# Running the last output blocks and the first input units token tile by token tile between the parts of a macaron decoder layer

## What is computed

```python
def sandwich(x, fn, g_pre, g_post, shift, scale, gate, res_w):
    h = rms_norm(x, g_pre) * (1.0 + scale[:, None]) + shift[:, None]
    y = rms_norm(fn(h), g_post)
    return x + res_w * gate[:, None] * y

x = sandwich(x, lambda h: swiglu(h, ffn1_w_in[l], ffn1_w_out[l]), ...)
x = sandwich(x, lambda h: token_mixer(h, ...), ...)      # attention, sparse attention, retention
x = sandwich(x, lambda h: swiglu(h, ffn2_w_in[l], ffn2_w_out[l]), ...)
```

## Time and profile before

| | |
|---|---|
| three runs | 2011.61, 2013.59, 2013.87 us, median 2013.59 us |
| the profiled execution | 2008.18 us, its span 2006.1 us |
| TensorE busy | 1903.8 us, 95% of the span |
| VectorE busy | 1413.9 us, 70% |
| ScalarE busy | 825.3 us, 41% |
| mean granted clock of TensorE | 0.976 |

### The profile page before, as it was taken

The page is one execution under the profiler, slowest core; times in us unless marked ns, Lnnn a source line. Parts: engine busy times, 40 slices in busy tenths (PEclk is TensorE's granted clock), DMA queues, the critical chain, the costliest instruction groups (busy, mean ns, idle before and its releaser), DMA issues.

```text
span 2006.1 us, 21422 instructions
## 1 busy us (share of the span) xinstructions
PE 1903.8 (95%) x8610; PEld 1549.7 (77%) x8610; DVE 1413.9 (70%) x1474; ACT 825.3 (41%) x1019; POOL 20.0 (1%) x24
## 2 busy tenths in 40 slices
PE   2779999999999999899999999899999999999996
PEld 2558878878878788777777787788888888888895
DVE  5997888888878878765766567656656665555556
ACT  2224434443444343344565534443444444443442
POOL 0000000000000000000000000000000000000000
PEclk6789999999999999999999999999999999999998
DMA  9889988989989989435333435366666665555551
GB/s 347 321 313 351 354 338 324 357 325 343 346 322 347 347 327 340 162 114 184 126 115 129 156 133 187 135 243 231 246 243 232 235 218 189 189 189 189 195 194 73
DMA packets 204129, 486.82 MB, mean 243 GB/s; under 512 B 8048, under 2 KB 21120, under 8 KB 188928
## 3 DMA queue, kind: packets, MB, share of 16 engines
q1 hardware_dynamic: 202816, 482.79, 66.4%
q10 hardware_dynamic: 992, 2.63, 0.4%
...
...
## 4 chain that ended last, share of the span: by engine, by line
PE 49%; issue 38%; DVE 6%; DMA 2%; ACT 1%; POOL 0%; SPq 0%; POOLq 0%; DVEq 0%; ACTq 0%
PE ps_u L1328 6%; PE ps_g L1328 6%; PE ps_u L1330 5%; PE ps_u L1329 5%; PE ps_g L1330 5%; PE ps_g L1329 5%; DMA ada_raw<-in_ada_w 2%; DVE arena L1086 2%; PE ps_t L1328 2%; PE ps_t L1329 2%; PE ps_t L1330 2%; PE ps_y L1328 2%; PE ps_y L1330 2%; PE ps_y L1329 2%; DVE w_lo L812 1%
## 5 line engine op out<-in xcount | busy, mean ns | idle before, releaser
L812 DVE TENSOR_TENSOR w_lo<-w_raw,w_hi 128x1024 fp32r<-128x1024 f32 (+1 forms) x632 | 753.0, 1200 | 491.0 <-ACT w_hi L485 489.9
L485 ACT ACTIVATE w_hi<-w_raw 128x1024 fp32r<-128x1024 f32 (+1 forms) x632 | 657.2, 1042 | 944.6 <-PE ps_u L1330 336.1
L1328 PE MATMUL ps_u<-w_hi,xT_hi 128*128 128x512 f32 (+2 forms) x880 | 349.5, 397 | 19.5 <-DVE w_lo L812 18.7
L1328 PE MATMUL ps_g<-w_hi,xT_hi 128*128 128x512 f32 (+1 forms) x880 | 347.5, 395 | 18.4 <-DVE w_lo L812 9.6
L1329 PE MATMUL ps_u<-w_lo,xT_hi 128*128 128x512 f32 (+2 forms) x880 | 342.5, 389 | 0.0
L1330 PE MATMUL ps_u<-w_hi,xT_lo 128*128 128x512 f32 (+2 forms) x880 | 342.4, 389 | 0.0
L1330 PE MATMUL ps_g<-w_hi,xT_lo 128*128 128x512 f32 (+1 forms) x880 | 342.2, 389 | 0.0
L1329 PE MATMUL ps_g<-w_lo,xT_hi 128*128 128x512 f32 (+1 forms) x880 | 341.8, 388 | 0.0
L836 DVE SCALAR_TENSOR_TENSOR arena<-ada_raw,cond,arena 128x2048 f32<-128x2048 f32 x108 | 253.4, 2346 | 19.1 <-DMA ada_raw<-in_ada_w 19.0
L1328 PEld LDWEIGHTS ps_g<-w_hi,xT_hi 128*128 128x128 f32 x880 | 166.5, 189 | 61.0 <-issue 15.8
L1328 PEld LDWEIGHTS ps_u<-w_hi,xT_hi 128*128 128x128 f32 x880 | 167.7, 191 | 58.6 <-DVE w_lo L812 22.2
...
## 6 DMA issues: line engine op xcount, KB each, us to landing
w_raw<-in_ffn_w_in SPq DMA_DIRECT2D x160, 1024.0 KB, 5.0
ada_raw<-in_ada_w SPq DMA_DIRECT2D x128, 1024.0 KB, 7.1
w_raw<-in_ffn_w_out SPq DMA_DIRECT2D x80, 1024.0 KB, 5.0
w_raw<-in_mix_w_in SPq DMA_DIRECT2D x32, 1024.0 KB, 5.0
arena<-in_ada_w SPq DMA_DIRECT2D x16, 1024.0 KB, 10.2
w_raw<-in_mix_w_out SPq DMA_DIRECT2D x16, 1024.0 KB, 5.0
...
```

Of the source, the lines that this page charges most:

```text
L485: nc.scalar.activation(w_hi[:, u % 4, 0:n, 0:width], w_raw[:, s, 2 * hf:2 * hf + n, 0:width], ACT.Copy).then_inc(hi_done, 1)
L812: nc.vector.tensor_tensor(w_lo[:, u % 4, 0:n, 0:width], w_raw[:, s, 2 * hf:2 * hf + n, 0:width], w_hi[:, u % 4, 0:n, 0:width].bitcast(F32) ...
L1328: nc.tensor.matmul(o, a_hi[:, k, rows], w_hi[:, b, c, 0:width], start=start, stop=False)
```

## The change

The last two output blocks of a part (b = 2, 3) are computed for tile 0 of both, then for tile 1 of both (`last_blocks`), and the first four units of the next part's first group for tile 0, then for tile 1 (`first_group`). The norm steps of a turn are done per tile in one function `turn` on ScalarE and one on VectorE. The transposes of x come as eight pieces of 128 tokens for the first half of the chunks (`x_part`, `xt_part`) and as pairs for the second half. Scale and shift move from VectorE (L1021) to ScalarE: two activations with a scale and a bias column each, from PSUM into `junk`, then after a wait on its own semaphore a copy into `xT_hi` (`scaled`, `xt_hi_part`, `xt_hi_pair`). The identity matmuls become 20, then 16 after the first square of x. The last hidden block of a feed-forward part is transposed after output block 1 of the group before, into `ps_g`, and its split lands in `xT_hi` and `xT_lo`. The powers are four per turn instead of two (two instead of one at the end).

```diff
+            def xt_hi_part(n, b, t):
+
+                if b == 0 and t == 0:
+                    act.wait_ge(modcol_done, STRIPS + 2 * n)
+                    act.wait_ge(ysq_done, SQ_PART * n)
+                act.wait_ge(xt_done, 8 * n + 2 * t + b // 2 + 1)
+                raw = raw_part(b, t)
+                scaled(n, b, raw, xt_part(b, t), P)
+                nc.scalar.activation(xT_hi[:, 2 * b:2 * b + 2, t * P:(t + 1) * P], raw.rearrange("p (c n) -> p c n", n=P),
+                                     ACT.Copy).then_inc(xt_hi_done, 1)
...
+            def turn(n, y0, g, width):
+
+                sq = SQ_PART * n
+                for b in range(2):
+                    act.wait_ge(y_added, y0 + b + 1)
+                    y_square(n, b, 0, 2 * b)
+                    y_square(n, b, 1, 2 * b + 1).then_inc(ysq_done, 1)
+                act.wait_ge(ysq_done, sq + 2)
+                for b in (2, 3):
+                    act.wait_ge(y_first, 2 * n + b - 1)
+                    y_square(n, b, 0, b - 2).then_inc(ysq_done, 1)
+                if g is not None:
+                    hi_group(g, 4, width, None, range(0, 1))
+                    x_square(n + 1, 0, 0)
+                    x_square(n + 1, 0, 1)
+                for b in (2, 3):
+                    act.wait_ge(y_added, y0 + b + 1)
+                    y_square(n, b, 1, b).then_inc(ysq_done, 1)
+                if g is None:
+                    return
+                hi_group(g, 4, width, None, range(1, 2))
+                xt_hi_part(n + 1, 0, 0)
+                xt_hi_part(n + 1, 1, 0)
+                hi_group(g, 4, width, None, range(2, 3))
+                x_square(n + 1, 1, 0)
+                xt_hi_part(n + 1, 2, 0)
+                x_square(n + 1, 1, 1)
+                hi_group(g, 4, width, None, range(3, 4))
+                xt_hi_part(n + 1, 3, 0)
                 for b in range(4):
-                    xt_hi_later(n, b)()
+                    xt_hi_part(n + 1, b, 1)
+                for b in range(4, 8):
+                    hi_group(g, 4, width, None, range(b, b + 1))
+                    xt_hi_pair(n + 1, b)
 
 
...
@@ -925,7 +969,7 @@
                 last = FBLOCKS - 1
                 hidden(last, g0 + 5 + 3 * LOOP, TAIL)
                 yl, gy = y0 + 4 * last, g0 + 8 + 3 * LOOP
-                tail = {0: [y_add(gy - 1, yl - 2, 2)], 2: [y_add(gy - 1, yl - 1, 3)], 3: [ht_lo(j0 + last, TAIL // P)],
+                tail = {0: [ht_lo(j0 + last, TAIL // P, xT_hi, xT_lo, ps_g), y_add(gy - 1, yl - 2, 2)], 2: [y_add(gy - 1, yl - 1, 3)],
                         4: [gates(2 * f, 1 if f == 0 else 3, 0.5)], 5: [y_add(gy, yl, 0)], 7: [y_add(gy, yl + 1, 1)]}
                 lo_group(gy, TAIL // P, NB, tail)
...
-                    lo_group(g_next, 4, NB, None, range(0, 1))
-                y_add(g, y0 + 2, 2, False, pairs)()
-                if g_next is not None:
-                    lo_group(g_next, 4, NB, None, range(1, 2))
-                gated(2)
-                if g_next is not None:
-                    lo_group(g_next, 4, NB, None, range(2, 3))
-                last = slice(3 * NB, 4 * NB)
-                dve.wait_ge(y_added, y0 + 3)
-                dve.wait_ge(pe_half, n + 1)
-                nc.vector.tensor_tensor(yacc[:, 0, last], pairs[1][:, 0, :], yacc[:, 0, last], ALU.add).then_inc(y_first, 1)
-                dve.wait_ge(pe_used, 8 * g + 8)
-                nc.vector.tensor_tensor(yacc[:, 1, last], pairs[1][:, 1, :], yacc[:, 1, last], ALU.add).then_inc(y_added, 1)
-                dve.wait_ge(ysq_done, 4 * n + 4)
-                link(nc.vector.reduce_sum(ss[:, 0:2], ssy[:, :, :], AX_X))
-                nc.vector.tensor_scalar(ss[:, 0:2], ss[:, 0:2], 1.0 / D, EPS, ALU.mult, ALU.add).then_inc(var_ready, 1)
-                norms[0] += 1
-                gated(3)
-                dve.wait_ge(rstd_ready, norms[0])
-                dve.wait_ge(y_gated, 4 * n + 4)
-                for t in range(TILES):
-                    for part in range(2):
-                        cols = slice(part * D // 2, (part + 1) * D // 2)
-                        nc.vector.scalar_tensor_tensor(x_sb[:, t, cols], yacc[:, t, cols], rstd[:, t:t + 1], x_sb[:, t, cols],
-                                                       ALU.mult, ALU.add).then_inc(x_new, 1)
+                last_add(2, 0)
+                gated(2, 0)
+                last_add(3, 0)
+                dve.wait_ge(ysq_done, sq + 4)
+                y_first_ready = variance(0, ssy[:, 0:1, :])
+                gated(3, 0)
+                x_update(0, 0, y_first_ready)
+                x_update(0, 1, y_first_ready)
+                last_add(2, 1)
+                last_add(3, 1)
+                if gn is None:
+                    gated(2, 1)
+                    dve.wait_ge(ysq_done, sq + 6)
+                    y_second_ready = variance(1, ssy[:, 1:2, :])
+                    gated(3, 1)
+                    x_update(1, 0, y_second_ready)
+                    x_update(1, 1, y_second_ready)
+                    return
+                dve.wait_ge(xsq_done, 2 + 4 * n + 2)
+                x_first_ready = variance(2, ssx[:, 0:1, :])
+                gated(2, 1)
+                x_normal(0, 0, x_first_ready)
+                dve.wait_ge(ysq_done, sq + 6)
+                y_second_ready = variance(1, ssy[:, 1:2, :])
+                lo_group(gn, 4, width, None, range(0, 1))
+                gated(3, 1)
+                xt_rest(0, 0)
+                x_update(1, 0, y_second_ready)
+                lo_group(gn, 4, width, None, range(1, 2))
+                xt_rest(1, 0)
+                x_update(1, 1, y_second_ready)
+                lo_group(gn, 4, width, None, range(2, 3))
+                xt_rest(2, 0)
+                dve.wait_ge(xsq_done, 2 + 4 * n + 4)
+                x_second_ready = variance(3, ssx[:, 1:2, :])
+                lo_group(gn, 4, width, None, range(3, 4))
+                x_normal(1, 0, x_second_ready)
+                xt_rest(3, 0)
+                x_normal(0, 1, x_first_ready)
+                x_normal(1, 1, x_second_ready)
+                for b in range(4):
+                    xt_rest(b, 1)
+                for b in range(4, 8):
+                    lo_group(gn, 4, width, None, range(b, b + 1))
+                    xt_rest(b)
 
             def input_scale(n, meanwhile=None):
...
+            def last_blocks(g, a_hi, a_lo, chunk0, chunks, y0, pairs):
+
+                for t in range(TILES):
+                    for n in (2, 3):
+                        ps = pairs[n % 2]
+                        if t == 0:
+                            pe.wait_ge(y_added, y0 + n - 1)
+                        for hf in range(2):
+                            m = min(2, chunks - 2 * hf)
+                            pe.wait_ge(lo_done, 8 * g + 2 * n + hf + 1)
+                            ins = half_unit(a_hi, a_lo, chunk0 + 2 * hf, (2 * n + hf) % 4, m, NB, ps[:, t, :], t, hf == 0, hf == 1)
+                            if t == 1:
+                                ins.then_inc(pe_used, 1)
+                            elif hf == 1:
+                                ins.then_inc(pe_half, 1)
...
+            def x_part(n, t):
+
+                pe.wait_ge(xn_ready, 4 * (n - 1) + t + 1)
+                for b in range(4):
+                    for c in range(2):
+                        k = 2 * b + c
+                        ins = nc.tensor.transpose(xt_part(b, t)[:, c * P:(c + 1) * P], yacc[:, t, k * P:(k + 1) * P], ident[:, :])
+                    if b % 2:
+                        ins.then_inc(xt_done, 1)
...
+            def first_group(n, g, width, ps, ps_warm):
+
+
                 pe.wait_ge(gates_ready, n)
-                warm(24, ps)
-                pe.wait_ge(x_new, 4 * (n - 1) + 1)
-                warm(18, ps)
-                pe.wait_ge(xsq_done, 2 + 4 * n)
-                warm(8, ps)
-                for b in range(3):
-                    x_pair(n, b)()
-
-            def xt_pairs(n):
-                return {b - 3: [x_pair(n, b)] for b in range(3, 8)}
+                warm(20, ps_warm)
+                pe.wait_ge(xsq_done, 2 + 4 * (n - 1) + 1)
+                warm(16, ps_warm)
+                x_part(n, 0)
+                for t in range(TILES):
+                    for b in range(4):
+                        if t == 0 and b == 3:
+                            x_part(n, 1)
+                        if t == 0:
+                            pe.wait_ge(lo_done, 8 * g + b + 1)
+                        pe.wait_ge(xt_lo_done, xt_count(n, b, t))
+                        ins = half_unit(xT_hi, xT_lo, 2 * b, b, 2, width, ps[:, t, 0:width], t, b == 0, False)
+                        if t == 1:
+                            ins.then_inc(pe_used, 1)
+                            x_pair(n, 4 + b)
+                for b in range(4, 8):
+                    pe.wait_ge(lo_done, 8 * g + b + 1)
+                    pe.wait_ge(xt_lo_done, xt_count(n, b))
```

(12 more changed lines are left out.)

301 lines of the change are left out of this document (136 added, 165 removed).

## The result

The changed kernel takes 1992.33 us (median of 4 runs, 1989.65 to 1994.62) against 2012.6 us for the kernel before on the same chip (4 runs): a ratio of 0.9898, 95% interval 0.9886 to 0.991. It is 20.3 us faster. The forecast was 1997.8 us with a range from 1993.5, so the direction and the places were right, but the time lies 5.5 us under the forecast and 1.2 us under the range. The profiled execution took 1992.25 us, its span is 1990.5 us.

What follows compares the result with a forecast made beforehand. TensorE, busy 95% of the span, bounds the kernel except in a few places. First turn -9.5, second -5.6, end -0.7, together -15.8 us: 2008.18 becomes 1992.4 profiled, 1997.8 us on the median; range 1993.5 to 2003.5.

Steps and rivals of the forecast that it cites:

- the early transposes: Both feed-forward tails: transposing the last hidden block earlier removes the wait for `hT_lo`, gain 1.9 us each.
- the wait for block 1's add: Last output blocks: new TensorE wait before block 3 of tile 0, 0.8 us first turn, 1.0 to 1.1 second.
- the identity matmuls, not the norm, set the start: After the last block: 72 identity matmuls, 8.3 us, delay the transposes; in the first turn both end within 0.7 us.
- from the blocks' end: Last block to first weight matmul: 10.9 us instead of 20.81 and 19.07, so -9.9 and -8.2 us.
- The overlaps of neighbours: Overlaps within one queue, left out, about 0.9 us a turn; held against one half-speed stretch in one turn (1.7).
- VectorE's last chain: Kernel end, block 1's add to last update: 18.0 us, or 17.8 with some overlap, against 16.62 before.
- A pair of scaled activations: ScalarE, before the first weight matmul: two activations with scale and bias columns, 0.48 us each, 0.96 together.
- The three waits in the group: First group, tile 0 half: TensorE waits 1.5 us twice, then 1.3; group 29.0 us, +1.5 each turn.
- the clock's second case: Clock rival: neither turn pays for a half-speed stretch and overlaps count, 1996.0 us; no separate chance given.
- The case with 1994.5 us: Neither turn pays for the clock, activations at their lower bound, 0.75 us a turn less; 1993 to 1995.8, chance 0.20.
- both turns pay: Clock rival: half-speed stretches cost time in both turns, 1999.8 us; dearer activations or this, 2000 to 2003.5, chance 0.17.
- on the median, 5.41 us above it: Base of the sum: the median lies 5.41 us above the profiled execution, turning 1992.4 into 1997.8 us.

## Why the forecast missed the time, and what of it held

The bound, the places and the mechanism held. Of the steps by their own numbers: the early transposes gave 1.95 us in each tail for 1.9; the wait for block 1's add cost 0.82 and 1.13 for 0.8 and 1.0 to 1.1; the identity matmuls, not the norm, set the start in both turns, which the runs with fewer of them show (3.0 us gained in the second turn); from the blocks' end it was 10.61 us for 10.9; VectorE paced tile 0's half.

The failed step is in the sum: "The overlaps of neighbours that I left out, about 0.9 us a turn, are held against one such stretch in one of the turns (1.7)". No stretch came in a turn, and the overlaps were real, so that 2.2 us of gain were missing (18.0 for 15.8). By terms, of which I can place these: 0.3 and 0.3 up to the first weight matmul, nearly all of it because the identity matmuls took 8.04 us for 8.3; 0.35 and 0.3 in the groups, where the step from one half unit to the next was 2.67 us for 2.85, twice; 0.6 in VectorE's last chain (17.2 for 17.8: from the reduction to the first update it was 1.38 us where I had 2.0, since GpSimd's power of one column took 0.92); 0.4 in small places. A pair of scaled activations took 0.79 us for 0.96, 0.10 of it by their overlap, but from the transposes to the first weight matmul it was 2.57 us for 2.6, so other links of that chain were longer. The three waits in the group were 1.04, 1.04 and 0.87 us and not 1.3 to 1.5: a half unit behind a wait takes 1.63 us from start to end (2.67 - 1.04), not 1.36.

Of the rivals, the clock's second case was the right one: neither turn paid and the overlaps counted. It had a gain of 17.6 us (1996.0), and the stages have 18.0. The case with 1994.5 us is nearer to the measured median, but by luck: it takes the activations at their lower bound of 0.40 and 0.50 us, and single ones took 0.45 and 0.55. The Trainium skill, "TensorE: Matmul & The Clock Gate", Part 4: PE-mode transpose, says that transposes do not count for the clock as matmuls do, from which the prediction had both turns pay. The trace of the changed kernel has eight transposes between waits in each turn and a clock of 1.00, so here both turns did not pay as long as identity matmuls ran ahead of them. No run puts matmuls in the place of the transposes, so the rule itself is not tested. One reading of the prediction was wrong: there was not one half-speed window in each turn but two in the first, as shown above.

The second failed step is the base: "on the median, 5.41 us above it". The median of three runs was 2013.59; over the 70 timed executions of before on record it is 2012.3 us. That is 1.3 us. The remaining 2.0 us (20.0 between 2012.3 and 1992.3, the median of eight executions of after, less 18.0) are in no stage of the profiles of the two kernels, and their cause stays open. About 0.2 us lie outside the span: the time is 1.97 us above the span on the mean in before and 1.79 in after. What is shown is that a half-speed stretch of 1.5 to 1.7 us comes or stays away from one execution to the next at places where TensorE waits for 2 us: in the mixer in 5 of 11 profiles with the changed turns that kept the wait, and in a tail of before in one. The change removes the two waits in the tails, so before can lose time there that after can't. That this is the rest of the 2.0 us is argued and not shown; the three profiles of the unchanged kernel before had no such stretch in the mixer or the tails. The rival is the opening, whose mean over four profiles of before is too uncertain to exclude it.

Against my account of the change speaks its second part: the tile order of the last two blocks was costed as a loss of TensorE's time (+0.8 and +1.1) that buys an earlier chain. The loss was right; the gain isn't there.
